# Down projection of fifteen experts by seven block products, in the mixture-of-experts phase of a denoising layer

## The chip, the cores and the metric

The kernel runs on one core of one Trainium2 chip. Its engines work side by side, each through its own list of instructions, and wait for one another by semaphores: TensorE (PE, matmuls into PSUM), ScalarE (ACT), VectorE (DVE), GpSimd (POOL, which also issues the gathers and scatters), and SyncE (SP), which issues most loads. The metric is the device time of one execution of the whole kernel, in microseconds; lower is better.

## The reference, cut to what matters

The layer has a mixer (a long convolution and a retention branch) and then a mixture of experts. Only the experts and the last norm are touched here. `T` is 2048 for the latent tokens and 128 for the context tokens, `D` is 1024, there are 16 experts, and each takes its own best tokens: 256 latent and 16 context ones.

```python
def ec_moe(h, p):
    xt = h.reshape(T, D)
    aff = jax.nn.softmax((xt @ p["w_router"]).astype(F32), axis=-1)
    cap = (EC_CAPACITY_FACTOR * T) // N_EXPERTS
    vals, idx = lax.top_k(aff.T, cap)
    xs = xt[idx]
    hid = jax.nn.silu(einsum("ecd,edf->ecf", xs, w_e_gate)) * einsum("ecd,edf->ecf", xs, w_e_up)
    ye = jnp.einsum("ecf,efd->ecd", hid, p["w_e_down"]) * vals[..., None]
    y = jnp.zeros((T, D)).at[idx.reshape(-1)].add(ye.reshape(-1, D))
# trunk_layer:  x = x + g2 * ec_moe(h, p);   result: rmsnorm(x, norm_f_g)
```

## The kernel before, in words

The kernel has seven phases, one after the other: filters, tokens, hyena input, middle, merge, out, experts. The experts phase (`phase_experts`, L2804) is about the last 1245 us. The merge phase, which the diff leaves alone, has sums of weight and row blocks on GpSimd in its own right (L2401 to L2425) and low parts on VectorE (L2302).

All products with large weights are made from three matmuls of rounded operands (`product`, L71 to L73): each float32 operand is split in a high part, rounded to fp32r, and a low part, the rest. high x high, high x low and low x high are added up in PSUM. ScalarE writes a high part (`split` in the scalar block, L3150), VectorE then the low part (`split` in the vector block, L3374: raw minus high).

An expert has 24 weight rows of 128x1024, streamed in the order of the list `STREAM`: for each f of 8 a gate column g_f, an up column u_f and, one f later, a down row d_f. SP loads them (`loads`). TensorE makes g_f and u_f for 272 slots (`column`, 8 x 3 matmuls of 272 columns each); ScalarE applies silu to g_f (`act_g`, L3197); VectorE multiplies with u_f to the hidden row `full` (L3467, 256 latent slots) and `full_c` (L3468, 16 context slots); ScalarE rounds `full` (L3208) and VectorE takes its low part (L3476), with a split of a weight row between the two. Then `down` (TensorE) adds the row f of the down projection to four PSUM banks: two halves of the slots by two halves of the 1024 output columns, 4 x 3 matmuls of 512 columns for a row, 96 for an expert. The rows 0 to 5 lie between the columns of the same expert; `down_context` (L3093, the 16 context slots straight from the raw rows) follows after u7, and rows 6 and 7 after that. Four gatings on VectorE (L3501: PSUM x routing value x gate) write `ye`, and a context gating (L3489). GpSimd scatters `ye` onto the residual in memory (L3611), waits until it has landed (`carry`, L3535), and then gathers the tokens of the next expert that is due (L3548 to L3557).

Beside this, VectorE counts positions for the expert after the next (`passed`, L3334 and L3337), and it and ScalarE split the transposed tokens of the next expert (`turned`; L3380 and L3383 from PSUM). In the last expert the final norm of all 17 tiles runs between the columns: GpSimd loads tiles of the residual, ScalarE squares them (L3170), VectorE scales them (L3408), GpSimd stores them. This starts when the scatter of expert 14 has landed. The rows which expert 15 itself adds to are gathered, added to and stored at the end (L3414, L3423, L3596).

The order on each engine is written out by hand in its `body`, called 16 times by `experts`. A weight row is split two stream positions ahead of its use (`LEAD`).

## Time and profile before

| | |
|---|---|
| median of three timed runs | 3281.8 us (3281.4 to 3283.2) |
| the profiled execution | 3281.0 us, its span 3279.1 us |
| mean granted TensorE clock | 0.965 of full |
| PE busy | 3086.5 us (94%) |
| DVE busy | 1910.9 us (58%) |
| ACT busy | 1412.6 us (43%) |
| POOL busy | 525.5 us (16%) |
| DMA | 630.7 MB, mean 192 GB/s |

A busy share is the time in which an engine works on an instruction; issuing DMAs and waiting for semaphores is not counted. The span goes from the first to the last instruction. The granted clock is the share of TensorE's full clock that the chip lets it have: 1.00 is 2.4 GHz, 0.50 is 1.2 GHz. The ends of matmuls are modelled, so that the distance between their starts, and not their duration, is the cost of one in a run of them.

### The profile page before, as it was taken

The numbers are of one execution on the slowest core, as the hardware profiler recorded it, in microseconds if no ns is written. First come the engines' busy times: TensorE is split into PE (matmuls) and PEld (weight loads), VectorE is DVE, ScalarE is ACT, GpSimd is POOL, SyncE is SP. The second block draws the span as 40 slices with busy tenths as digits, with TensorE's granted clock in tenths as the row PEclk, the third lists the DMA queues.
The fourth block names the chain that finished last, engine by engine and source line by source line (L and its number), as shares of the span: only waits on it lengthen the run. The fifth ranks groups of instructions, "written<-read, shape, count | busy, mean of one in ns | idle before, by whom it ended". The sixth has DMA issues, their size and how long they took to land. (4 is left out here: it accounts for less than half of the span.)

```text
span 3279.1 us, 52938 instructions
## 1 busy us (share of the span) xinstructions
PE 3086.5 (94%) x20253; PEld 2673.8 (82%) x20253; DVE 1910.9 (58%) x3135; ACT 1412.6 (43%) x2101; POOL 525.5 (16%) x440
## 2 busy tenths in 40 slices
PE   7899999899979879999999994999999999999997
PEld 2478888799945779999997773999999999899996
DVE  5544443433345578776755558666666666666656
ACT  4633333422234145564644541444444444444446
POOL 1011111000023344101000003121111111112212
PEclk9999999999989889999999995999999999999998
DMA  8733332422199976767655443565555555565668
GB/s 332 262 110 119 121 108 88 153 60 63 54 326 357 338 236 219 244 212 236 211 175 196 160 147 120 197 208 201 192 197 195 187 190 182 182 207 194 198 207 310
DMA packets 338341, 630.73 MB, mean 192 GB/s; under 512 B 28408, under 2 KB 209912, under 8 KB 333961
## 3 DMA queue, kind: packets, MB, share of 16 engines
q1 hardware_dynamic: 312159, 568.47, 50.8%
q0 software_dynamic: 16992, 54.88, 5.7%
q10 hardware_dynamic: 8976, 4.46, 0.5%
q8 instruction: 143, 2.34, 0.3%
q14 instruction: 71, 0.58, 0.1%
HBM read 490.16 MB, written 137.56 MB: 191 GB/s over the span
## 5 line engine op out<-in xcount | busy, mean ns | idle before, releaser
L71 PE MATMUL experts_bank<-experts_xT_high,experts_w_high_gu 128*128 128x272 f32 x2048 | 595.4, 291 | 7.5 <-DVE experts_w_low_gu L3374 3.5
L73 PE MATMUL experts_bank<-experts_xT_high,experts_w_low_gu 128*128 128x272 f32 x2048 | 590.7, 288 | 0.0
L72 PE MATMUL experts_bank<-experts_xT_low,experts_w_high_gu 128*128 128x272 f32 x2048 | 588.8, 287 | 0.0
L71 PEld LDWEIGHTS experts_bank<-experts_xT_high,experts_w_high_gu 128*128 128x128 f32 x2048 | 385.5, 188 | 14.0 <-ACT experts_act_g L3197 6.3
L72 PEld LDWEIGHTS experts_bank<-experts_xT_low,experts_w_high_gu 128*128 128x128 f32 x2048 | 386.4, 189 | 4.6
L73 PEld LDWEIGHTS experts_bank<-experts_xT_high,experts_w_low_gu 128*128 128x128 f32 x2048 | 385.3, 188 | 0.0
L3374 DVE TENSOR_TENSOR experts_w_low_gu<-experts_w_raw_gu,experts_w_high_gu 128x1024 fp32r<-128x1024 f32 x256 | 302.3, 1217 | 24.9 <-ACT experts_w_high_gu L3150 20.1
L2145 PE MATMUL merge_bank<-merge_rows_high,merge_w_gates_high 128*128 128x272 f32 x896 | 261.5, 292 | 9.2 <-DVE merge_rows_low L2302 5.9
L3150 ACT ACTIVATE experts_w_high_gu<-experts_w_raw_gu 128x1024 fp32r<-128x1024 f32 x256 | 256.7, 1045 | 13.8 <-DMA experts_w_raw_gu<-in_w_stream 13.8
L2147 PE MATMUL merge_bank<-merge_rows_high,merge_w_gates_low 128*128 128x272 f32 x896 | 260.7, 291 | 0.0
L2146 PE MATMUL merge_bank<-merge_rows_low,merge_w_gates_high 128*128 128x272 f32 x896 | 259.3, 289 | 0.0
L73 PE MATMUL experts_bank<-experts_w_high_d,experts_hid_low 128*128 128x512 f32 x512 | 203.7, 398 | 0.0
L71 PE MATMUL experts_bank<-experts_w_high_d,experts_hid_high 128*128 128x512 f32 x512 | 203.6, 398 | 0.0
L3197 ACT ACTIVATE experts_act_g<-experts_bank 128x272 f32<-128x272 f32 x128 | 50.9, 397 | 352.4 <-PE experts_bank L73 352.4
L72 PE MATMUL experts_bank<-experts_w_low_d,experts_hid_high 128*128 128x512 f32 x512 | 202.3, 395 | 0.0
L3467 DVE TENSOR_TENSOR experts_full<-experts_bank,experts_act_g 128x256 f32<-128x256 f32 x128 | 54.4, 425 | 252.8 <-issue 150.3
L71 PE MATMUL hyin_pz<-hyin_hT_high,hyin_w_high 128*128 128x436 f32 (+1 forms) x480 | 176.3, 367 | 14.0 <-DVE hyin_hT_low L1421 14.0
L2145 PEld LDWEIGHTS merge_bank<-merge_rows_high,merge_w_gates_high 128*128 128x128 f32 x896 | 170.2, 190 | 9.9 <-issue 9.9
L3535 POOL TENSOR_TENSOR experts_spare<-experts_spare 128x1 f32<-128x1 f32 x46 | 29.5, 653 | 920.9 <-DVE experts_ye L3501 772.5
L72 PE MATMUL hyin_pz<-hyin_hT_low,hyin_w_high 128*128 128x436 f32 (+1 forms) x480 | 172.9, 360 | 0.0
L73 PE MATMUL hyin_pz<-hyin_hT_high,hyin_w_low 128*128 128x436 f32 (+1 forms) x480 | 172.9, 360 | 0.0
L2146 PEld LDWEIGHTS merge_bank<-merge_rows_low,merge_w_gates_high 128*128 128x128 f32 x896 | 170.4, 190 | 0.0
(435 smaller groups left out, 7257.9 us busy)
## 6 DMA issues: line engine op xcount, KB each, us to landing
experts_w_raw_gu<-in_w_stream SPq DMA_DIRECT2D x256, 512.0 KB, 4.6
experts_w_raw_d<-in_w_stream SPq DMA_DIRECT2D x128, 512.0 KB, 6.9
merge_rows_b<-scratch_hT SPq DMA_DIRECT2D x52, 544.0 KB, 5.1
filters_wm<-in_w_mod SPq DMA_DIRECT2D x12, 2048.0 KB, 10.8
merge_rows_t<-scratch_row_sums SPq DMA_DIRECT2D x36, 544.0 KB, 6.6
merge_y<-scratch_yhy SPq DMA_DIRECT2D x32, 544.0 KB, 5.1
merge_y<-scratch_yret SPq DMA_DIRECT2D x32, 544.0 KB, 4.6
x_early<-in_xT SPq DMA_DIRECT2D x17, 512.0 KB, 5.1
```

The costliest lines, as they stand in the source:

```text
L71: pe.matmul(out, lhs[0], rhs[0], start=start, stop=False)
L72: pe.matmul(out, lhs[0], rhs[1], start=False, stop=False)
L73: return pe.matmul(out, lhs[1], rhs[0], start=False, stop=stop)
L2145: pe.matmul(out, high, rh[:, w, q, :], start=not onto and q == 0, stop=False, skip_group_check=onto)
L2146: pe.matmul(out, high, rl[:, w, q, :], start=False, stop=False, skip_group_check=onto)
L2147: mm = pe.matmul(out, low, rh[:, w, q, :], start=False, stop=q == HK - 1, skip_group_check=onto)
L3150: act.activation(wh[kind][:, n % RINGS[kind], :], raw[kind][:, r, :], ACT.Copy).then_inc(*AW.inc(name))
L3197: act.activation(act_g[:], pg[:, 0:SLOTS], ACT.Silu).then_inc(*AG.inc(f"g{f}"))
L3374: v.tensor_tensor(wl[kind][:, w, :], raw[kind][:, n % STAGES[kind], :], wh[kind][:, w, :].bitcast(F32), ALU.subtract).then_inc(*VW.inc(name))
L3467: v.tensor_tensor(full[:, f % 2, :], pu[:, 0:CAP], act_g[:, 0:CAP], ALU.mult).then_inc(*VG.inc(f"m{f}"))
L3535: g.tensor_tensor(spare[:, column:column + 1], spare[:, 0:1], spare[:, 0:1], ALU.add)\
```

## The change

For experts 0 to 14 the down projection is made by Strassen's scheme in Winograd's form. The hidden matrix (256 slots by 1024) and the down weight (1024 by 1024) are cut in halves both ways. With A for hidden, B for weight: S1 = A21 + A22, S2 = S1 - A11, S3 = A11 - A21, S4 = A12 - S2; t1 = b12 - b11, t2 = b22 - t1, t3 = b22 - b12, t4 = b21 - t2. The seven products A11 b11, A12 b21, S1 t1, S2 t2, S3 t3, A22 t4, S4 b22 have 4 x 3 matmuls of 512 columns each, 84 for an expert.

- All seven products of expert e are moved behind columns 0, 1, 3, 5, 6, 7 and 8 of expert e+1 (`BEHIND`). Three PSUM banks hold them; four products add onto a bank that is already in use, after ScalarE has copied out its state (`copied`), and VectorE adds and gates the quarters (`evicted`, `summed`, `gated`).
- GpSimd makes t1, t3, t2 and t4 from the raw rows, in place: each is 4 rows of 512 columns, 128x2048 elements (`block_sum`, `quarter`). t1 stands ahead of the gather, the others between the gather and the scatter, which is now that of expert e-1.
- ScalarE and VectorE split 14 operand parts of 2 x 512 (`PARTS`), in the place of 8 rows, in a ring of three (`RING_D`, four before), most of them in expert e+1 (`SPLIT_AT`), three at the end of expert e (`SPLIT_NEXT`).
- VectorE makes S1 to S4 for f of 4 to 7, 16 sums of 128x128, and the low parts of 6 x 128 columns at once; for f of 0 to 3 only A11 (128 columns) is split.
- SP reloads the raw down rows after their last use (`load_row`), at positions 6 to 9 of the next expert.
- Expert 15 keeps the 96 matmuls, with its rows behind columns 11 to 15 and after. The final norm's batches, buffers and positions are changed (`BATCHES`, `SPOT`, `SQUARES`, `SCALED`).
- The context gating takes four pieces straight from PSUM on VectorE and one scaling on ScalarE.

The diff, cut to its core:

```diff
+STREAM = [f"{n}{f}" for f in range(KT) for n in "gu"]
+LEAD, RING, RING_D = 2, 4, 3
+HALF = KT // 2
+OPERANDS = ["b11", "b21", "t1", "t2", "t3", "t4", "b22"]
+PARTS = [f"{name}{i}" for name in OPERANDS for i in range(2)]
+BEHIND = {0: 0, 1: 1, 3: 2, 5: 3, 6: 4, 7: 5, 8: 6}
+SPLIT_AT = {1: [3], 2: [4, 5], 4: [6, 7], 5: [8], 6: [9, 10], 7: [11, 12], 8: [13]}
+SPLIT_NEXT = {13: 0, 14: 1, 15: 2}
+D_FIRST = (1, 6, 7, 8)
...
+        BATCHES = [(0, 4), (4, 8), (8, 12), (12, NT)]
+        SQUARES = {12: (0, 4), 14: (4, 8)}
+        SCALED = {13: (0, 4), 15: (4, 8)}
+        ROWS_AT = {6: (0, 1), 7: (2, 3), 8: (4, 5), 9: (6, 7)}
+        PASSED_AT = {0: (0, 6), 1: (6, 9), 3: (9, 13), 5: (13, NLAT)}
+        DOWN_AT = {11: 0, 12: 1, 13: 2, 14: 3, 15: 4}
...
+                def load_row(e, f):
+                    if e:
+                        sp.wait_ge(VP.sem, VP.at(e - 1, f"{'b22' if f >= HALF else 't3'}{f % HALF // 2}"))
+                        sp.wait_ge(TP.sem, TP.at(e - 1, "t4"))
...
+                def block_product(e, j):
+
+                    to = pd[:, (0, 1, 2, 0, 0, 0, 2)[j], :]
+                    onto = j > 2
...
+                    for i in range(2):
+                        n = 2 * j + i
+                        w = ring_d(e, n)
+                        pe.wait_ge(VP.sem, VP.at(e, PARTS[n]))
+                        for q in (2 * i, 2 * i + 1):
+                            high, low = hh[:, q, j, :], hl[:, q, j, :]
+                            right = slice(512 * (q % 2), 512 * (q % 2) + 512)
+                            pe.matmul(to, high, dh[:, w, right], start=not onto and q == 0, stop=False, skip_group_check=onto)
+                            pe.matmul(to, high, dl[:, w, right], start=False, stop=False, skip_group_check=onto)
+                            mm = pe.matmul(to, low, dh[:, w, right], start=False, stop=q == HALF - 1, skip_group_check=onto)
...
+                        if e and i == 2:
+                            copied(e - 1, 0, "p1")
+                        if e and i == 6:
+                            copied(e - 1, 3, "u2")
+                        if e and i == 7:
+                            copied(e - 1, 4, "u3")
...
+                def summed(e, c, j, name, done):
+
+                    to = {"c11": ye[:, 0, 0:512], "c22": ye[:, 1, 512:DM], "c12": ye[:, 0, 512:DM]}[done]
+                    v.wait_ge(DP.sem, DP.at(e, PARTS[2 * j + 1]))
+                    v.wait_ge(AY.sem, AY.at(e, name))
+                    v.tensor_tensor(to, pd[:, 1 if done == "c11" else 2, :], to, ALU.add).then_inc(*VD.inc(c))
+                    v.wait_ge(VD.sem, VD.at(e, c))
+                    gated(e, to, to, done)
...
+                    v.tensor_tensor(sums[:, 3, :], full[:, q, 0, :], full[:, q, 1, :], ALU.subtract).then_inc(*VG.inc(f"x{f}"))
+                    done("m")
+                    v.tensor_tensor(sums[:, 1, :], full[:, q, 1, :], sums[:, 4, :], ALU.add).then_inc(*VG.inc(f"z{f}"))
+                    done("z")
+                    v.tensor_tensor(sums[:, 2, :], sums[:, 1, :], full[:, q, 0, :], ALU.subtract).then_inc(*VG.inc(f"y{f}"))
+                    done("y")
+                    v.tensor_tensor(sums[:, 5, :], sums[:, 0, :], sums[:, 2, :], ALU.subtract).then_inc(*VG.inc(f"w{f}"))
...
+                def block_sum(e, name):
+
+                    if name == "t1":
+                        for f in range(HALF):
+                            g.wait_ge(dld[f], 16 * (e + 1))
+                        g.wait_ge(PC.sem, PC.at(e, "context"))
+                        g.wait_ge(VP.sem, VP.at(e, "b111"))
+                        to, a, b = quarter("b11"), quarter("t3"), quarter("b11")
...
+                    elif name == "t2":
+                        g.wait_ge(VP.sem, VP.at(e, "t11"))
+                        to, a, b = quarter("t2"), quarter("b22"), quarter("t1")
+                    else:
+                        g.wait_ge(TP.sem, TP.at(e, "t2"))
+                        g.wait_ge(VP.sem, VP.at(e, "b211"))
+                        to, a, b = quarter("t4"), quarter("b21"), quarter("t2")
+                    g.tensor_tensor(to, a, b, ALU.subtract).then_inc(*TP.inc(name))
...
                 def body(e, h, k, one, two):
-                    if final(e):
-                        finish(h)
-                        return
+                    if e:
+                        block_sum(e - 1, "t1")
                     if one:
                         gather(e + 1, 1 - h)
...
+                    if e:
+                        for name in ("t3", "t2", "t4"):
+                            block_sum(e - 1, name)
+                        scatter(e - 1)
+                    if final(e):
+                        finish(e % 3)
```

## Rows read from the trace of the kernel before

**Rows 1.** Windows, one expert each: us, busy of each engine, clock, DMA share, GB/s
```profile
core 0: us, PE busy (x) PEld busy (x) DVE busy (x) ACT busy (x) POOL busy (x), PEclk, DMA share, GB/s
2563.60:2639.90 76.30, 76.30 (x567) 70.01 (x568) 47.91 (x83) 33.48 (x51) 14.87 (x12) 1.00 0.58 196
...
3097.40:3173.50 76.10, 76.10 (x563) 69.82 (x562) 41.63 (x65) 33.32 (x50) 14.00 (x12) 1.00 0.59 196
3173.50:3279.00 105.50, 83.10 (x568) 73.34 (x568) 68.88 (x87) 63.20 (x101) 31.30 (x45) 0.92 0.83 301
```

**Rows 2.** Chain of waits: start us, us, engine, tile, line
```profile
2033.68 0.60 PE experts_bank L71
...
2106.04 0.34 PE experts_bank L71
...
2604.85 0.44 PE experts_bank L3052 x4
2614.09 0.44 PE experts_bank L3052 x4
...
3173.47 0.43 PE experts_bank L71
```

**Rows 3.** Timeline of TensorE in the down rows: start us, us, instruction
```profile
2564.01 0.39 PE L73 MATMUL experts_bank<-experts_w_high_d,experts_hid_low 128*128 128x512 f32 x1
...
2568.91 0.39 PE L73 MATMUL experts_bank<-experts_w_high_d,experts_hid_low 128*128 128x512 f32 x1
```

**Rows 4.** Groups of VectorE, one expert (2563.6 to 2639.9): busy us, mean ns, idle before
```profile
L3374 DVE TENSOR_TENSOR experts_w_low_gu<-experts_w_raw_gu,experts_w_high_gu 128x1024 fp32r<-128x1024 f32 x16 | 18.9, 1218 | 0.0
...
L3476 DVE TENSOR_TENSOR experts_hid_low<-experts_full,experts_hid_high 128x256 fp32r<-128x256 f32 x8 | 3.3, 418 | 0.0
L3501 DVE SCALAR_TENSOR_TENSOR experts_ye<-experts_bank,experts_vals,experts_gate 128x512 f32<-128x512 f32 x4 | 2.8, 749 | 1.0 <-PE experts_bank L73 1.0
L3383 DVE TENSOR_TENSOR experts_xT_low<-experts_bank,experts_xT_high 128x512 fp32r<-128x512 f32 x4 | 2.8, 690 | 7.3 <-ACT experts_xT_high L3162 7.3
...
L3489 DVE SCALAR_TENSOR_TENSOR experts_ye<-experts_ye,experts_vals,experts_gate 16x1024 f32<-16x1024 f32 x1 | 1.3, 1271 | 1.1 <-ACT experts_ye L3217 1.1
...
L3380 DVE TENSOR_TENSOR experts_xT_low<-experts_bank,experts_xT_high 128x128 fp32r<-128x128 f32 x1 | 0.3, 290 | 1.0 <-ACT experts_xT_high L3161 1.0
```

**Rows 5.** Timeline of VectorE in the same expert
```profile
2570.00 2.35 DVE L3374 TENSOR_TENSOR experts_w_low_gu<-experts_w_raw_gu,experts_w_high_gu 128x1024 fp32r<-128x1024 f32 x2
```

**Rows 6.** Groups of ScalarE in the same expert
```profile
L3150 ACT ACTIVATE experts_w_high_gu<-experts_w_raw_gu 128x1024 fp32r<-128x1024 f32 x16 | 16.0, 1044 | 0.0
...
L3208 ACT ACTIVATE experts_hid_high<-experts_full 128x256 fp32r<-128x256 f32 x8 | 3.4, 419 | 16.4 <-DVE experts_full L3467 16.4
```

**Rows 7.** Groups of GpSimd over the span, two sums of the merge phase's first blocks
```profile
L1958 POOL TENSOR_TENSOR merge_rows_b<-merge_rows_b,merge_rows_b 128x1088 f32<-128x1088 f32 x1 | 2.5, 2474 | 0.0
L1948 POOL TENSOR_TENSOR merge_gates_sum<-merge_gates 128x1024 f32<-128x1024 f32 x1 | 2.3, 2342 | 0.0
```

**Rows 8.** Timeline of VectorE in the merge phase, 1362 to 1380
```profile
1365.28 3.11 DVE L2302 TENSOR_TENSOR merge_rows_low<-merge_rows_b,merge_rows_high 128x1088 fp32r<-128x1088 f32 x1 [1.77 <-ACT merge_rows_high L2224]
1368.32 0.77 DVE L2319 TENSOR_TENSOR merge_gate<-merge_bank,merge_sums 128x272 f32<-128x272 f32 x2
...
1378.55 1.28 DVE L2302 TENSOR_TENSOR merge_rows_low<-merge_y,merge_rows_high 128x1088 fp32r<-128x1088 f32 x1
```

**Rows 9.** Timeline of GpSimd over the same stretch
```profile
1364.85 2.39 POOL L2419 TENSOR_TENSOR merge_gates_sum<-merge_gates 128x1024 f32<-128x1024 f32 x1 [74.16 <-DMA merge_gates<-in_w_gates]
1367.32 3.33 POOL L2421 TENSOR_TENSOR merge_gates_sum<-merge_gates_sum,merge_gates 128x1024 f32<-128x1024 f32 x1
```

**Rows 10.** Groups of GpSimd in one expert (2563.6 to 2639.9), the gather's affinity rows
```profile
L3557 POOL DMA_INDIRECT experts_aff_rows<-scratch_aff,experts_ids x3 | 4.0, 1330 | 0.9 <-issue 0.9
```

**Rows 11.** Windows of the merge phase while four sums run on GpSimd (columns as rows 1)
```profile
1205.00:1210.00 5.00, 0.54 (x5) 0.32 (x3) 1.79 (x1) 2.68 (x4) 4.87 (x3) 1.00 0.66 237
1210.00:1215.00 5.00, 3.72 (x16) 3.75 (x17) 5.00 (x6) 2.20 (x3) 5.00 (x2) 0.57 0.64 181
```

**Rows 12.** Timeline of GpSimd in the last expert: the carry behind the scatter
```profile
3195.70 0.19 POOL L3535 TENSOR_TENSOR experts_spare<-experts_spare 128x1 f32<-128x1 f32 x1 [7.50 <-DMA scratch_xacc<-experts_ye,experts_sids]
```

622 lines of the change are left out of this document (378 added, 244 removed).

## The prediction

> **What bounds the kernel now.** I began with the page's busy shares and then left them, since a mean over seven phases says little about one. The first view that counts is the table of windows, one window for each expert [rows 1]. In a middle expert TensorE is busy for all of the 76.3 us at a granted clock of 1.00; VectorE is busy for 47.9 us, ScalarE for 33.5 and GpSimd for 14.9. The chain of waits over the same stretches passes through TensorE alone: the first down product behind the context rows of expert 0 starts at 2106.04 and that of expert 14 at 3173.47, so an expert takes 1067.43 / 14 = 76.25 us [rows 2]. In the timeline the 512-column matmuls of the down projection start 0.233 us apart (21 steps from 2564.01 to 2568.91) [rows 3]. Two transpose groups stand 9.24 us apart in the chain, and between them lie two columns, one down row of 12 matmuls and the transposes [rows 2]: (9.24 - 2.80 - 0.44) / 2 = 3.00 us for one gate or up column. So TensorE is the bound, with no idle time, in experts 1 to 14, and in the last expert it is not: there it is busy for 83.1 of 105.5 us while the final norm runs [rows 1].
>
> **What the change takes from TensorE.** The down projection of an expert has 96 matmuls of 512 columns now (8 rows, 4 outputs, 3 terms). Seven products of 4 rows and 3 terms are 84. 12 x 0.233 = 2.80 us less for each of 15 experts, 42.0 us in all, if TensorE stays the bound: 73.5 us an expert. All else on TensorE (columns, transposes, context, index) is only reordered.
>
> **What it puts on VectorE, for one expert.** The rows are those of one expert's window [rows 4]; an instruction that follows another without a wait costs less than its mean, as two splits take 2.35 us together in the timeline against 1.22 for one [rows 4, 5], so 1.13 each.
> - Weight parts: 14 splits in the place of 8, 6 x 1.13 = +6.8 us.
> - Hidden rows: the low part is 128 wide for four rows and 768 wide for the other four, where it was 256. From 256 to 1024 elements the rows go from 418 to 1218 ns, 1.04 ns an element: 4 x 0.53 - 4 x 0.13 = +1.6 us.
> - Sums of hidden halves: 16 instructions of 128 elements, in a chain of waits on itself. No row has this form with both inputs in SBUF; the nearest is the 128-element subtraction of 290 ns. 16 x 0.29 = +4.6 us (bounds 0.20 and 0.35 each, 3.2 to 5.6).
> - Evictions: 3 additions from PSUM (690 ns by the 512-element subtraction from PSUM) and 4 gatings (749 ns) for 4 gatings now: about +2.3 us with the longer issue of single ones. The context's four pieces of 256 elements (418 ns by the row of that width) replace one of 1271 ns: +0.4.
> Together 47.9 + 15.7 = 63.6 us. To that comes a wait that VectorE has not now: between the product `full` and its low part it ran a weight split while ScalarE rounded, and now the two stand next to each other. ScalarE's 256 elements take 419 ns and 1024 take 1044 [rows 6], so 768 take 0.84 and 128 about 0.3. With 0.1 for the semaphore this is 4 x 0.95 + 4 x 0.3 = 5.0 us. 68.6 us: by itself that would still fit under 73.5.
>
> **The four weight sums on GpSimd decide it.** Each has 128x2048 elements with two inputs in SBUF. The merge phase has such sums: undisturbed, 2342 ns for 1024 and 2474 for 1088 elements [rows 7]. By the slope (2.06 ns an element) 2048 take 4.45 us, by doubling 4.68; I take 4.55, so 18.2 us an expert. What they do to VectorE is seen in two timelines of the merge phase. A VectorE subtraction of 1088 elements takes 1.28 us at 1378.55, when no sum runs. The one that begins at 1365.28, shortly after a GpSimd sum (1364.85 to 1367.24), takes 3.11 us: it ends at 1368.39, 1.15 us after the sum. The next sum starts at 1367.32 and takes 3.33 us instead of 2.34; it ends 2.26 us after that subtraction [rows 8, 9]. So instructions with two SBUF inputs exclude each other on these two engines, each for the whole length of the other. The page "SBUF — State Buffer" of the Trainium skill (Who interferes with whom) adds that a VectorE instruction with one SBUF input is free of this; the trace agrees, since the two of L2319 at 1368.32, which read PSUM, take 0.77 us within the sum [rows 8, 9]. No row has a sum of 2048 elements. The Trainium skill's page "GPSIMD Engine Reference" (Elementwise — side-by-side cycle accounting) gives 4497 ns for one, by which the four would be 18.0 us instead of my 18.2; its section Engine selection says to keep elementwise work off GpSimd, which speaks against this part of the change.
>
> Nearly everything VectorE does here has two SBUF inputs: the 30 splits, the 14 counting steps L3337, the hidden sums, the low parts. Only `full`, the additions from PSUM, the xT parts and the waits for ScalarE can lie beside a sum. All four sums fall in the first half of an expert, by their place: t1 when the context product is over, then the gather of the next expert (three instructions of 1.33 us [rows 10] and three like them, some 8 us with the gaps), then t3, t2, t4 one behind the other. With the durations above, in the order of the code, from TensorE's start of an expert: t1 0.1 to 4.6, VectorE blocked at the last low part of the expert before; then context pieces and numbers to 7.3; split gu2, six counting steps 10.8; splits d3, gu3, three steps 14.3; `full` 0 14.9; t3 14.6 to 19.1, low 0 blocked to 19.4; splits gu4, d4, d5 22.8, gu5 24.0; t2 24.0 to 28.5 (it needs d5), gating c11 blocked to 29.2; t4 29.2 to 33.7, four counting steps blocked to 35.3; `full` 1 35.9. So 15.8 of the 18.2 us are lost and 2.4 lie beside something. u2 needs the PSUM bank that `full` 1 frees: TensorE would take it up at 27.5 and stands for some 8 us. The merge phase has such a place: while its sums run, TensorE is busy 0.54 of 5 us, and the granted clock is 0.57 in the next stretch, most of it at the level of 1.2 GHz [rows 11]. That comes on top and costs a later column up to 3 us. VectorE's own round is then 68.6 + 15.8 = 84.4, and it waits 2 to 3 us for TensorE and ScalarE at the products: **86.5 us an expert** instead of 76.3 (the walk itself, with each row's mean, closes at 88). TensorE's 42 us turn into idle time.
>
> Bounds of this period: 77.5 if the sums lie beside all the waits and all the PSUM reads (8 us beside) and the hidden sums cost 0.2 each; 91 if every stall brings the low clock and TensorE then is late for VectorE in its turn. I take 86.5 by the walk.
>
> **Other edits.** ScalarE gets 6 splits (+6.0), wider rounding (+1.3) and three copies (+1.8) and stays near 43 us; costed at nothing, but its copies p1, u2, u3 stand ahead of its splits, and while one waits for a product the splits behind it wait too; that is in the 2 to 3 us. SP now waits for the last part of b22 and for t4 before it reloads the down rows; behind that wait stand the gate and up loads, which have four columns (12 us) of room: nothing, unless the wait is longer than that; then TensorE waits for a column. The scatter moves from the start of the next expert to about 65 us into it and ends before the next t1: nothing in the middle, but it costs at the end.
>
> **The ends.** Expert 0 does six of its down rows before its context product now (2033.68 to 2106.04, 72.4 us [rows 2]); after the change they go to the next expert: 72.4 - 6 x 2.8 = 55.6. Expert 14 has no counting steps (41.6 against 47.9 us of VectorE [rows 1]): 80.5 us. The last expert takes 105.6 now, from 3173.47. Its final norm starts after the scatter of expert 14, whose carry ends at 3195.9, 22 us in [rows 12]; the two down rows (5.6) and the last gating before it leave some 15 us for the scatter and its landing. After the change it needs the last product of expert 14, at about 59 us, and ends at 74. Then 4 tiles land (5), ScalarE squares them ahead of its next splits (5 to 7), then two columns and rows 4 to 7 of the last down projection follow with stalls (about 25), and after the last product VectorE still has 9 tiles to scale (1.2 each), 3 row groups and 4 gatings (about 27): 74 + 12 + 25 + 27 = 138 us. TensorE's own minimum is 105.6 + 14.0 = 120 (seven products of expert 14 for two rows of it); bounds 122 and 150.
>
> **Sum.** Now the phase takes 72.4 + 1067.4 + 105.6 = 1245.4 us. After: 55.6 + 13 x 86.5 + 80.5 + 138 = 1398.6, +153. On the profiled span 3279.1 that is 3432; the profiled execution lies 1.9 us above its span and 0.8 below the median: 3435 us. With the low bounds (77.5, 73.5, 122) it is 3296, with the high ones (91, 85, 150) 3510.
>
> **Rivals.**
> 1. Faster, with TensorE still the bound. The 4 sums must then cost VectorE less than 73.5 - 68.6 = 4.9 us an expert, and less than 7.7 for any gain in the period at all. For it: VectorE is idle 28 us an expert now, much of it before hidden rows. Against: these gaps are filled by 20 us of new work, and the merge phase shows no sum that costs so little. Its time is 3281.8 - 42 + 18 for the tail = 3258. 12%.
> 2. The exclusion is there, but half of it is hidden, if VectorE runs ahead of TensorE when a sum comes, or if the sums fall on its waits for ScalarE (5 us). For it: t1 comes where VectorE now waits for the last columns. Against: t3, t2 and t4 follow each other, with 11 down splits due in the same 40 us. Period 79: 13 x 79 + 76 + 130 + 56 = 1289, +44: 3326. 15%.
> 3. The gain and the lock cancel: period 75 to 76, within 0.2% of now: 2%.
> 4. The forecast, 83 to 91 an expert, 3385 to 3510 in all: 71%.
> Range: 3315 to 3495 leaves out the faster case (12 to 13%) and the last 7%. About 0.2% (6.6 us) is what a measurement of this kernel tells from no change: faster 0.13, same 0.02, slower 0.85.
>
> **What would show it.** By windows: a middle expert of 86 us, VectorE busy for all but 5 to 8 us of it, TensorE idle 12 or more. By lines: the four sums at 4.5 to 5.8 us each, the 1024-element low splits with a mean well over 1.22 (some at 4 to 5.7). In the waits: TensorE on `full_context` or on the low splits. The granted clock under 1.00 in the first half. Wrong would be: all low splits at 1.22 us while a sum runs, or a period of 73.5 with VectorE under 68 us.

## The result, and the profile after

The changed kernel takes 3534.8 us (median; 3532.1 to 3537.0) against 3281.6 for the kernel before: a ratio of 1.0768, 95% interval 1.0755 to 1.0781. The profiled execution has a span of 3531.7 us and a mean granted clock of 0.941. The forecast was 3435 us with a range of 3315 to 3495: the direction was right, and the size was short by 100 us.

The page of the kernel after: busy time of each engine, then the groups that grew (busy us, mean ns of one | idle before, and what ended it).

```profile
PE 3114.6 (88%) x20073; PEld 2694.8 (76%) x20073; DVE 2381.5 (67%) x3558; ACT 1512.1 (43%) x2184; POOL 805.5 (23%) x500
...
L3493 DVE TENSOR_TENSOR experts_w_low_gu<-experts_w_raw_gu,experts_w_high_gu 128x1024 fp32r<-128x1024 f32 x256 | 312.6, 1221 | 84.6 <-ACT experts_w_high_gu L3241 79.8
L3782 POOL TENSOR_TENSOR experts_w_raw_d<-experts_w_raw_d 128x2048 f32<-128x2048 f32 x60 | 293.7, 4895 | 276.8 <-PE experts_bank L3176 176.0
L3502 DVE TENSOR_TENSOR experts_w_low_d<-experts_w_raw_d,experts_w_high_d 128x1024 fp32r<-128x1024 f32 x210 | 251.2, 1220 | 51.2 <-ACT experts_w_high_d L3256 51.2
```

VectorE now waits 79.8 us for the high parts of the gate and up rows and 51.2 us for those of the down parts. Before, the same splits had an idle time of 0.0 ahead of them [rows 4].

Windows of a middle expert (from one chunk index instruction on VectorE to the next), of expert 14 and of the last expert (these two from the end of one context product on TensorE to the end of the next, the last one to the end of the span): us, busy of PE, PEld, DVE, ACT, POOL, granted clock, DMA share, GB/s.

```profile
2750.53:2843.14 92.61, 78.52 (x555) 71.72 (x554) 79.78 (x112) 40.36 (x56) 33.32 (x16) 0.93 0.50 161
3301.57:3386.60 85.03, 77.48 (x551) 70.15 (x550) 72.21 (x93) 40.44 (x56) 31.61 (x16) 0.96 0.54 173
3386.60:3531.70 145.10, 100.77 (x630) 87.98 (x628) 96.97 (x109) 70.71 (x106) 49.53 (x49) 0.85 0.61 217
```

These answer to [rows 1]. A middle expert took 76.3 us with TensorE busy throughout; now it takes 92.6, TensorE is idle for 14.1 of them, and VectorE has gone from 47.9 to 79.8 us. The same index instruction (the one which, in both kernels, stands at the start of an expert on VectorE) gives a split of the whole difference between the two spans:

| stretch, by that mark | before | after | difference | forecast |
|---|---|---|---|---|
| start to expert 1 | 2106.2 | 2099.3 | -6.9 | -16.8 |
| experts 1 to 13 | 991.4 | 1208.1 | +216.7 (16.7 each) | +133 (10.25 each) |
| experts 14 and 15, to the end | 181.5 | 224.4 | +42.9 | +36.7 |
| span | 3279.1 | 3531.7 | +252.6 | +153 |

So 83 of the missing 100 us lie in the period of the middle experts. How the rest is divided depends on the mark. In the changed kernel VectorE comes to the index instruction of expert 1 5.8 us after TensorE has ended the context product (2093.50 and 2099.28), since the sum t1 holds up the last low part; before, these two were 0.4 us apart (2105.83 and 2106.22). The forecast was made from TensorE's times. By these the start is 12.3 us shorter (forecast 16.8) and the last two experts are 48.2 us longer (forecast 36.7): 4 of the missing us at the start and 12 at the end.

Where VectorE's time goes in the middle expert of 92.6 us, by its groups:

```profile
L3493 DVE TENSOR_TENSOR experts_w_low_gu<-experts_w_raw_gu,experts_w_high_gu 128x1024 fp32r<-128x1024 f32 x16 | 19.5, 1220 | 4.1 <-ACT experts_w_high_gu L3241 4.1
L3502 DVE TENSOR_TENSOR experts_w_low_d<-experts_w_raw_d,experts_w_high_d 128x1024 fp32r<-128x1024 f32 x14 | 16.7, 1220 | 2.9 <-ACT experts_w_high_d L3256 2.9
L3457 DVE SCALAR_TENSOR_TENSOR experts_tally<-experts_pos_slot,experts_tally 128x256 bf16<-128x256 f32 x14 | 15.0, 1127 | 0.0
L3568 DVE TENSOR_TENSOR experts_hid_low<-experts_hid_sums,experts_hid_high 128x768 fp32r<-128x768 f32 x4 | 7.8, 1960 | 3.7 <-ACT experts_hid_high L3329 3.7
L3517 DVE SCALAR_TENSOR_TENSOR experts_ye<-experts_ye,experts_vals,experts_gate 128x512 f32<-128x512 f32 x3 | 5.9, 1957 | 0.1
```

The weight splits (first two rows) are not stretched at all: 1220 ns, as in [rows 4]. What is stretched are the counting steps (1127 ns), the 768-wide low parts (1960) and three gatings (1957). The timeline shows how. First GpSimd, then VectorE, in the first half of the next expert (start us, us, [idle before <- what ended it]):

```profile
2853.65 4.59 POOL L3782 TENSOR_TENSOR experts_w_raw_d<-experts_w_raw_d 128x2048 f32<-128x2048 f32 x1
2864.76 10.41 POOL L3782 TENSOR_TENSOR experts_w_raw_d<-experts_w_raw_d 128x2048 f32<-128x2048 f32 x2 [6.53 <-DVE experts_w_low_d L3502]
```

```profile
2852.81 6.12 DVE L3457 SCALAR_TENSOR_TENSOR experts_tally<-experts_pos_slot,experts_tally 128x256 bf16<-128x256 f32 x3
2858.96 0.42 DVE L3543 TENSOR_TENSOR experts_full<-experts_bank,experts_act_g 128x256 f32<-128x256 f32 x1
...
2861.19 1.23 DVE L3493 TENSOR_TENSOR experts_w_low_gu<-experts_w_raw_gu,experts_w_high_gu 128x1024 fp32r<-128x1024 f32 x1 [1.14 <-ACT experts_w_high_gu L3241]
...
2866.46 4.37 DVE L3517 SCALAR_TENSOR_TENSOR experts_ye<-experts_ye,experts_vals,experts_gate 128x512 f32<-128x512 f32 x1
2870.75 5.90 DVE L3457 SCALAR_TENSOR_TENSOR experts_tally<-experts_pos_slot,experts_tally 128x256 bf16<-128x256 f32 x4
```

The sum from 2853.65 to 2858.24 holds up three counting steps until 2858.93. Of the next pair of sums the first holds up a gating. When, by its length, this sum is through, the gating gets in for its own 0.7 us, and then the four counting steps wait out the second. TensorE, which needs the rows that VectorE makes, stops in its turn. The longest stop ends at 2877.12, and a lower clock follows it, as windows of 5 us show (columns as above):

```profile
2877.12 0.59 PE L71 MATMUL experts_bank<-experts_xT_high,experts_w_high_gu 128*128 128x272 f32 x1 [7.40 <-DVE experts_full_context L3544]
```

```profile
2870.60:2875.60 5.00, 0.00 (x0) 0.00 (x0) 5.00 (x3) 0.00 (x0) 4.58 (x1) 0.80 0.00 0
2875.60:2880.60 5.00, 3.48 (x16) 3.48 (x17) 4.05 (x9) 3.59 (x6) 0.00 (x0) 0.52 0.04 7
```

The wait of 1.14 us at 2861.19 is of the other kind. ScalarE, in the same stretch:

```profile
2848.38 1.04 ACT L3241 ACTIVATE experts_w_high_gu<-experts_w_raw_gu 128x1024 fp32r<-128x1024 f32 x1
2859.41 0.31 ACT L3325 ACTIVATE experts_hid_high<-experts_full 128x128 fp32r<-128x128 f32 x1 [10.00 <-DVE experts_full L3543]
2859.63 0.58 ACT L3263 ACTIVATE experts_ye<-experts_bank 128x512 f32<-128x512 f32 x1
2860.11 1.05 ACT L3241 ACTIVATE experts_w_high_gu<-experts_w_raw_gu 128x1024 fp32r<-128x1024 f32 x1
```

ScalarE stands idle for 10.00 us in front of the rounding of the hidden row, which needs VectorE's product. The high part of the next gate row (2860.11) is behind it in ScalarE's order. If only that order holds it back, it could have been made in those 10 us (a run below tests this). VectorE, the slower of the two, comes to the low part of that row at 2860.05 and waits for it.

The longest wait for a gate row stands at the start of the expert and is of the same kind. Here it is the scaling of the context rows (`ye`, L3337) that needs VectorE's pieces, and the first high gate part is behind it. ScalarE, then VectorE:

```profile
2845.06 1.15 ACT L3337 ACTIVATE experts_ye<-experts_ye,experts_vals 16x1024 f32<-16x1024 f32 x1 [6.97 <-DVE experts_ye L3682]
2846.21 1.04 ACT L3241 ACTIVATE experts_w_high_gu<-experts_w_raw_gu 128x1024 fp32r<-128x1024 f32 x1
```

```profile
2847.28 1.22 DVE L3493 TENSOR_TENSOR experts_w_low_gu<-experts_w_raw_gu,experts_w_high_gu 128x1024 fp32r<-128x1024 f32 x1 [2.26 <-ACT experts_w_high_gu L3241]
```

So of the 4.1 us that VectorE waits for gate rows in an expert, 2.3 stand behind the scaling of the context rows and 1.1 and 0.7 behind the rounding of a hidden row.

### The profile page after: what moved, and what is told of

It is laid out like the page before. It is cut to its first block and busy times, and to the rows that moved or that the text cites. A ratio compares the mean times of both kernels' runs of the same rounds, so it can differ in the third digit from the quotient of the medians.

```text
span 3531.7 us, 53322 instructions
## 1 busy us (share of the span) xinstructions
PE 3114.6 (88%) x20073; PEld 2694.8 (76%) x20073; DVE 2381.5 (67%) x3558; ACT 1512.1 (43%) x2184; POOL 805.5 (23%) x500
## 5 line engine op out<-in xcount | busy, mean ns | idle before, releaser
L71 PE MATMUL experts_bank<-experts_xT_high,experts_w_high_gu 128*128 128x272 f32 x2048 | 619.6, 303 | 116.5 <-DVE experts_full_context L3544 114.1
L72 PE MATMUL experts_bank<-experts_xT_low,experts_w_high_gu 128*128 128x272 f32 x2048 | 607.9, 297 | 0.0
L71 PEld LDWEIGHTS experts_bank<-experts_xT_high,experts_w_high_gu 128*128 128x128 f32 x2048 | 405.5, 198 | 134.9 <-DVE experts_full_context L3544 120.5
L72 PEld LDWEIGHTS experts_bank<-experts_xT_low,experts_w_high_gu 128*128 128x128 f32 x2048 | 405.4, 198 | 5.1
L3493 DVE TENSOR_TENSOR experts_w_low_gu<-experts_w_raw_gu,experts_w_high_gu 128x1024 fp32r<-128x1024 f32 x256 | 312.6, 1221 | 84.6 <-ACT experts_w_high_gu L3241 79.8
L3782 POOL TENSOR_TENSOR experts_w_raw_d<-experts_w_raw_d 128x2048 f32<-128x2048 f32 x60 | 293.7, 4895 | 276.8 <-PE experts_bank L3176 176.0
L3502 DVE TENSOR_TENSOR experts_w_low_d<-experts_w_raw_d,experts_w_high_d 128x1024 fp32r<-128x1024 f32 x210 | 251.2, 1220 | 51.2 <-ACT experts_w_high_d L3256 51.2
L3145 PE MATMUL experts_bank<-experts_w_high_d,experts_hid_high 128*128 128x512 f32 x420 | 176.8, 421 | 76.1 <-DVE experts_w_low_d L3502 76.0
L3256 ACT ACTIVATE experts_w_high_d<-experts_w_raw_d 128x1024 fp32r<-128x1024 f32 x210 | 214.0, 1047 | 0.0
L3457 DVE SCALAR_TENSOR_TENSOR experts_tally<-experts_pos_slot,experts_tally 128x256 bf16<-128x256 f32 x210 | 205.9, 1039 | 0.0
L3147 PE MATMUL experts_bank<-experts_w_high_d,experts_hid_low 128*128 128x512 f32 x420 | 171.9, 409 | 0.0
```

Of the source, the lines that this page charges most:

```text
L71: pe.matmul(out, lhs[0], rhs[0], start=start, stop=False)
L72: pe.matmul(out, lhs[0], rhs[1], start=False, stop=False)
L3145: pe.matmul(to, high, dh[:, w, right], start=not onto and q == 0, stop=False, skip_group_check=onto)
L3457: mm = v.scalar_tensor_tensor(mine, slot[:], at, mine, ALU.is_ge, ALU.add)
L3493: v.tensor_tensor(gl[:, w, :], raw_gu[:, w, :], gh[:, w, :].bitcast(F32), ALU.subtract).then_inc(*VW.inc(STREAM[n]))
L3502: v.tensor_tensor(rows(dl[:, w, :]), part_of(e, n), rows(dh[:, w, :].bitcast(F32)), ALU.subtract)\
```

## The experiments

The theory: VectorE's own round is the period. It is its work, plus the sums that shut it out for their length, plus the waits into which the two hand-written orders of ScalarE and VectorE force it. The rivals: the price of the sums lies in the stalls and low clock of TensorE rather than in VectorE's round; the price depends on where sums stand, not on how long they are; or the products themselves (more splits, sums and waits without any GpSimd) are what costs. All periods below are means over experts 1 to 13 by the mark used above.

**Without the sums.** GpSimd keeps each place, wait and signal, and computes one element a partition; t1 to t4 are then the raw blocks.

```diff
-                    g.tensor_tensor(to, a, b, ALU.subtract).then_inc(*TP.inc(name))
+                    k = 1 + ("t1", "t3", "t2", "t4").index(name)
+                    g.wait_ge(TP.sem, TP.at(e - 1, name))
+                    g.tensor_tensor(token[:, k:k + 1], token[:, 0:1], token[:, 0:1], ALU.subtract).then_inc(*TP.inc(name))
```

> The four sums of 128x2048 on GpSimd are left out (a subtraction of one element a partition stands in their place, with the same waits), so the weight operands t1 to t4 are the raw blocks. Exclusion theory: in the changed kernel VectorE's instructions are stretched by 16.7 us an expert while a sum runs; without them the period falls from 92.9 to 76 to 78 us, the time to about 3315 us (3290 to 3335), and the counting steps, the 768-wide low parts and the gatings are back at 0.48, 0.96 and 0.75 us. Rival, that VectorE's other new work and its waits for ScalarE are the bound and the sums lie in its idle time: period 88 us or more, 3470 us or more.

Measured: 3289.2 us, ratio 1.0021 (1.0011 to 1.0031), 1 us below the range that I had given. The period is 75.9. Window and groups of one expert of it:

```profile
2701.81:2777.66 75.85, 74.23 (x556) 67.97 (x555) 63.06 (x112) 40.37 (x56) 15.91 (x16) 1.00 0.59 197
```

```profile
L3494 DVE TENSOR_TENSOR experts_w_low_gu<-experts_w_raw_gu,experts_w_high_gu 128x1024 fp32r<-128x1024 f32 x16 | 19.5, 1220 | 4.1 <-ACT experts_w_high_gu L3242 4.1
L3503 DVE TENSOR_TENSOR experts_w_low_d<-experts_w_raw_d,experts_w_high_d 128x1024 fp32r<-128x1024 f32 x14 | 16.8, 1220 | 2.9 <-ACT experts_w_high_d L3257 2.9
L3458 DVE SCALAR_TENSOR_TENSOR experts_tally<-experts_pos_slot,experts_tally 128x256 bf16<-128x256 f32 x14 | 5.9, 480 | 0.0
L3569 DVE TENSOR_TENSOR experts_hid_low<-experts_hid_sums,experts_hid_high 128x768 fp32r<-128x768 f32 x4 | 3.8, 958 | 3.7 <-ACT experts_hid_high L3330 3.7
L3518 DVE SCALAR_TENSOR_TENSOR experts_ye<-experts_ye,experts_vals,experts_gate 128x512 f32<-128x512 f32 x3 | 2.3, 752 | 0.1
```

Counting steps are back at 480 ns, 768-wide low parts at 958 and gatings at 752. The sums took 9.1 us from the counting steps, 4.0 from the low parts and 3.6 from the gatings: 16.7 us, VectorE's 79.8 less 63.1. The period fell by 17.0. What the sums held of VectorE appears in full in the period, and only 0.3 us more does, though the clock went from 0.93 to 1.00 and TensorE lost its stops. VectorE's waits for ScalarE (4.1, 2.9, 3.7) are the same with and without sums, so they aren't an effect of them. They also close the account of VectorE: 63.1 of work, 4.1 + 2.9 + 3.7 + 1.2 (before the 128-wide low parts) of waits for ScalarE, 0.4 for TensorE make 75.4 of 75.85 us. TensorE, which has 73.3 us to do, isn't the bound even here.

**Half the sums.** Each of the four over two of its four rows, 128x1024; the other half of t1 to t4 stays raw.

```diff
-                    g.tensor_tensor(to, a, b, ALU.subtract).then_inc(*TP.inc(name))
+                    half = lambda x: x[:, 0:2, :]
+                    g.tensor_tensor(half(to), half(a), half(b), ALU.subtract).then_inc(*TP.inc(name))
```

> The changed kernel, with each of the four GpSimd sums over two of its four rows alone (128x1024 in the place of 128x2048; the other half of t1 to t4 stays raw). Exclusion theory: the cost goes by length. Taking the sums away gave 17.0 us an expert (92.9 to 75.9), so half of their length gives back 7 to 9: period about 85, 3415 us (3395 to 3440). Rival, that each of the four instructions costs by being there (the order of the two engines, the waits between the sums): 92, 3525 us.

Measured: 3400.8 us, 1.0356 (1.0338 to 1.0373), period 84.3. With four sums at the same places, half as long, the cost over the form without them is 8.4 us instead of 17.0. The cost goes by length; a price for each hand-over would have stayed.

**The sums on VectorE.** The four go to VectorE, ahead of the splits at columns 0, 3, 4 and 5.

```diff
+                SUM_AT = {0: "t1", 3: "t2", 4: "t3", 5: "t4"}
...
+                        if e and i in SUM_AT:
+                            block_sum(e - 1, SUM_AT[i])
                         for todo in splits(e, i):
```

> The same four sums, on VectorE in its own order (2.2 to 2.3 us each by 1.04 ns an element) instead of GpSimd. Exclusion theory: 9.1 us of work in the place of 16.7 us of blocked time, 7.6 us less in each of 14 experts: about 3430 us (3400 to 3460), though VectorE has more to do. Rival, that the sums on GpSimd cost VectorE nothing and VectorE is the bound by its own load: 9 us more in each expert, about 3660 us.

Measured: 3374.3 us, 1.028 (1.0263 to 1.0297), period 82.0. I had expected 3430 (3400 to 3460). So this was a miss: the gain is 161 us where I had expected 105.

```profile
L3553 DVE TENSOR_TENSOR experts_w_raw_d<-experts_w_raw_d 128x2048 f32<-128x2048 f32 x4 | 9.2, 2300 | 0.1
```

A sum takes VectorE 2.30 us, where GpSimd takes 4.6 and holds VectorE for nearly all of that. So the work costs less on the engine that is the bound than it does beside it. And of the 9.2 us only 6.1 reach the period: t1 at column 0 fills a wait for ScalarE (the waits of the gate and up splits go from 4.1 to 1.1 us). My forecast had left this wait out, and it makes 3.0 of the 3.3 us an expert by which it was short.

**The same sums beside a VectorE with room.** The kernel before, with eight subtractions of 128x1024 on GpSimd in each of experts 1 to 14, on an idle buffer, at the places of the four sums in GpSimd's order. This adds work and leaves the rest as it was.

```diff
+                    for i in range(2):
...
+                        g.tensor_tensor(spot[:], spot[:], spot[:], ALU.subtract).then_inc(*TP.inc(order[n]))
```

> The kernel before, with eight subtractions of 128x1024 on GpSimd in each of the experts 1 to 14, on a buffer that nothing else uses then, at the places where the changed kernel has its four sums; nothing needs their result. Exclusion theory: some of VectorE's splits take 3 to 3.5 us instead of 1.22, its busy time grows by 12 to 17 us an expert, but it has 28 us of idle time, so TensorE stays the bound: 3282 to 3300 us. Rival, that a sum on GpSimd costs its length wherever it stands: 18 us an expert, 3530 us.

Measured: 3307.1 us, 1.0068 (1.0051 to 1.0085), period 78.2 against 76.3. That is 7 us above the range that I had expected, and far from the rival's 3530. One expert of it, window and GpSimd's group:

```profile
2731.90:2809.87 77.97, 76.48 (x568) 69.97 (x567) 57.48 (x85) 33.25 (x51) 32.57 (x20) 1.00 0.57 191
```

```profile
L3613 POOL TENSOR_TENSOR experts_final_spot<-experts_final_spot 128x1024 f32<-128x1024 f32 x8 | 17.3, 2162 | 0.5
```

17.3 us of sums lengthen VectorE by 9.6 us (57.5 for 47.9) and the expert by 1.9. In the changed kernel 19.5 us of sums lengthen it by 16.7 and the expert by 17.0. Sums hold VectorE in both (two of the splits here take 2.91 us); what differs most is the 28 us of idle time that VectorE had here and doesn't have there. The run doesn't settle whether it matters where the sums fall: they have the same places in GpSimd's list, but not the same times, since these wait for none of VectorE's splits, and t1's place comes 23.1 us behind the mark here and 5.5 us ahead of it there. TensorE waits a little (1.5 us for a low part of the transposed tokens) and makes no stop that brings the clock down (1.00).

**ScalarE's order.** ScalarE makes the high part of the next gate column ahead of the rounding of the hidden row, not behind it. Behind the last hidden row of an expert this puts it ahead of the scaling of the context rows too.

```diff
                         for todo in splits(e, i):
-                            split(*todo)
+                            if i % 2 or todo[0] != "gu" or (e, i) == (0, 0):
+                                split(*todo)
+                        if i % 2 and e * NS + i + 1 < NE * NS:
+                            for todo in splits(*divmod(e * NS + i + 1, NS)):
+                                if todo[0] == "gu":
+                                    split(*todo)
```

> On ScalarE the high part of the next even column is made ahead of the rounding of the hidden row, not behind it. Ordering theory: of the 9.1 us an expert in which VectorE waits for ScalarE's high weight parts some 6 go away, 6 x 14 = 84 us, about 3450 us (3430 to 3475). Rival, that this idle time only covers blocked time and moves elsewhere (the sums alone set the period): 3515 to 3535 us.

Measured: 3471.7 us, 1.0577 (1.056 to 1.0595), period 88.7, 4.2 us less than in the changed kernel. In one expert of 88.7 us (2718.84 to 2807.57) the wait of 4.1 us for the gate and up rows is gone, and the one for the down parts is a little longer:

```profile
DVE experts_w_low_d L3507 <- ACT experts_w_high_d L3256: 3.6, 3, 1.9
```

```profile
L3498 DVE TENSOR_TENSOR experts_w_low_gu<-experts_w_raw_gu,experts_w_high_gu 128x1024 fp32r<-128x1024 f32 x16 | 19.5, 1221 | 0.0
```

No instruction was taken away; the order of ScalarE alone is worth 4.2 us an expert, 63 us in the kernel. I had expected 6 us an expert, and the time lies in the range that I gave (3430 to 3475).

**The wait after the hidden row filled too.** ScalarE's order as in the run before, and VectorE makes the low part of that column between `full` and its low part, as the kernel before did. Once with the sums on GpSimd, once with them on VectorE, once without them.

```diff
+                            if e * NS + i + 1 < NE * NS:
+                                for todo in splits(*divmod(e * NS + i + 1, NS)):
+                                    if todo[0] == "gu":
+                                        split(*todo)
                             low(e, f)
```

> The changed kernel, GpSimd sums kept. ScalarE as in the run with the early high part, and VectorE makes the low part of that column between the hidden row and its low part, where it waited for ScalarE. Ordering theory: beside the 4.2 us that the early high part gave, 3 to 4.5 of the 4.9 us of waits after the hidden rows go away: period 84.5 (83 to 87), 3415 us (3395 to 3450). Rival, that the sums then block more, since VectorE has less idle time for them to fall on: 88, 3460 us.

> Both: the sums on VectorE and the order of the run with the filled waits. VectorE's load is then 63.1 + 9.1 = 72.2 us and TensorE's 73.5, both near the bound: period 74 to 76, 3275 us (3262 to 3300), the tail some 25 us longer than in the kernel before. Rival, that the two loads together with the points where they meet make 78 or more: 3320 us.

> The filled order, and the sums left out as in the run without them (t1 to t4 are raw blocks). VectorE has 63 us, TensorE 73.5 us: if TensorE's own count is right, the period is 73.5 to 74 and the time 3255 to 3262 us: the 2.8 us an expert of the saved matmuls appear in full. Rival, that something else (a wait between products and copies, the clock) holds TensorE above its count: 75.9 as without the fill, 3289 us.

| | us | ratio | period | same sums, order as changed |
|---|---|---|---|---|
| sums on GpSimd | 3453.7 | 1.051 (1.0493 to 1.0528) | 87.4 | 92.9 |
| sums on VectorE | 3323.7 | 1.0124 (1.0107 to 1.0141) | 78.4 | 82.0 |
| no sums | 3253.9 | 0.9904 (0.9888 to 0.9921) | 73.3 | 75.9 |

Windows of one expert of each, in the order of the table:

```profile
2710.21:2796.87 86.66, 75.56 (x557) 69.53 (x556) 79.03 (x112) 41.08 (x56) 32.62 (x16) 0.96 0.52 172
```

```profile
2718.44:2796.63 78.19, 74.17 (x556) 68.08 (x555) 71.32 (x116) 41.18 (x56) 13.79 (x12) 1.00 0.58 191
```

```profile
2756.28:2829.56 73.28, 73.28 (x556) 68.05 (x555) 62.63 (x113) 41.35 (x56) 14.14 (x16) 1.00 0.64 204
```

Without sums TensorE is busy for all of 73.28 us at full clock, and the 13 periods are alike to 0.1 us. That is the 73.5 which the count of matmuls gave: Strassen's saving is real, once VectorE is out of its way. But that kernel leaves the sums out. The two whole forms were both slower than I had expected (3415 and 3275), by 39 and 49 us, and both came out near their rivals (3460 and 3320). With the sums on GpSimd the waits after the hidden rows (4.9 us) are gone, and the period falls by 1.3 us only. The rival's cause, that the sums then hold VectorE for longer, isn't what the trace shows: they hold it for 16.4 us (79.0 of the window less the 62.6 of the run without sums), where it was 16.7. New waits of 1.4, 1.0 and 0.5 us stand in the same window. With the sums on VectorE, its 71.3 us of work and 6.2 us of waits make the period.

The form with the sums on VectorE points further, for its work of 71.3 us would fit under TensorE's 73.3. Its timeline has only 0.4 us of idle time on VectorE in columns 0 to 5, and these waits in an expert, the longest of them (2.2 us) behind column 6:

```profile
DVE experts_w_low_d L3507 <- ACT experts_w_high_d L3256: 3.0, 3, 2.2
DVE experts_hid_sums L3570 <- issue: 1.4, 1, 1.4
DVE experts_xT_low L3603 <- ACT experts_xT_high L3269: 1.0, 2, 0.5
DVE experts_w_low_gu L3498 <- ACT experts_w_high_gu L3241: 0.5, 2, 0.3
```

**Counting steps into the waits.** From there, 7 of the 16 counting steps go from columns 0 to 5 to columns 9 to 12, and with them the one step for the context (`passed_context`). Nothing else is touched.

```diff
-        PASSED_AT = {0: (0, 6), 1: (6, 9), 3: (9, 13), 5: (13, NLAT)}
+        PASSED_AT = {0: (0, 4), 1: (4, 6), 3: (6, 8), 5: (8, 9), 9: (9, 12), 10: (12, 13), 11: (13, 14), 12: (14, NLAT)}
...
-                            if part == 5:
+                            if part == 12:
                                 passed_context(e + 2)
```

> The filled order with the sums on VectorE, and 7 of the 16 counting steps moved from columns 0 to 5, where VectorE has no idle time in the trace of that form, to columns 9 to 12, where it waits 1.40, 0.47, 0.26, 0.27, 0.48 and 0.25 us. Nothing is left out. Theory (VectorE's round, work 71.3 us plus the waits that the order leaves): the 7 steps, 3.1 us, go into those waits, the period falls from 78.3 to 75.5, and the kernel takes 3323.7 - 13 x 2.8 = 3287 us. Rival: the waits of the second half are TensorE's pace and not room, and the period stays at 78 or falls by under 1 us: 3310 to 3324.

Measured: 3282.5 us, 0.9996 (0.9987 to 1.0005), which isn't told from no change, and period 75.3. The steps, 3.1 us by their length, took 3.1 us out of the period, from 78.4.

**The copy first.** In addition ScalarE copies u2 ahead of the rounding of the third hidden row.

```diff
-                        if e and i == 6:
-                            copied(e - 1, 3, "u2")
...
+                            if e and i == 5:
+                                copied(e - 1, 3, "u2")
```

> The same, and ScalarE copies u2 out ahead of the rounding of the third hidden row, not behind it. Nothing is left out. In the form without this TensorE waits 2.0 us an expert for a copy. Theory (in-order hand-overs on ScalarE): 1 to 2 us less an expert than with the counting steps moved alone, 3265 to 3275 us, which would be faster than the kernel before by 0.3 to 0.5%. Rival: the rounding is then late by as much, behind the product, and VectorE waits instead: no change, or up to 1 us an expert more.

Measured: 3273.9 us, 0.9973 (0.9963 to 0.9982), period 74.8. TensorE's wait for the copy (0.9 us) is gone; its wait for a low part goes from 0.5 to 1.2 us, and 0.5 us of period is all that comes of the edit.

**Counting steps ahead of the longest wait.** VectorE still waits 2.19 us for a high down part behind column 6. Five of the steps go there (the line with a minus is that of the run before this one).

```diff
-        PASSED_AT = {0: (0, 4), 1: (4, 6), 3: (6, 8), 5: (8, 9), 9: (9, 12), 10: (12, 13), 11: (13, 14), 12: (14, NLAT)}
+        PASSED_AT = {0: (0, 3), 3: (3, 4), 6: (4, 9), 9: (9, 12), 10: (12, 13), 11: (13, 14), 12: (14, NLAT)}
```

> The form with the copy first, and of the 9 counting steps still in columns 0 to 5 five are moved behind column 6, just ahead of the two down splits of column 7, where VectorE waits 2.19 us for ScalarE. Nothing is left out. Theory (VectorE's round is its work and the waits of the order): 5 steps of 0.42 us fill that wait, and the period falls by 1.2 to 1.5 us from 74.8 and stops at TensorE's own 73.3 to 73.6: 3273.9 - 13 x 1.3 = 3257 us, 3254 to 3260. Rival: the wait of 2.19 us is TensorE's pace (the ring slot of a product comes free late) and passes on to the next split: the period stays at 74.8 and the time at 3270 to 3276.

Measured: 3254.5 us (3253.3 to 3255.7), 0.9914 (0.9901 to 0.9928), period 73.3 in all 13. This form leaves nothing out and is faster than both kernels, than the one before by 0.86%. Window, then VectorE's groups of the down splits and of the sums:

```profile
2753.55:2826.84 73.29, 73.29 (x556) 68.06 (x556) 70.92 (x117) 41.28 (x56) 16.42 (x12) 1.00 0.63 204
```

```profile
L3507 DVE TENSOR_TENSOR experts_w_low_d<-experts_w_raw_d,experts_w_high_d 128x1024 fp32r<-128x1024 f32 x14 | 16.7, 1217 | 1.1 <-ACT experts_w_high_d L3256 1.1
L3558 DVE TENSOR_TENSOR experts_w_raw_d<-experts_w_raw_d 128x2048 f32<-128x2048 f32 x4 | 9.2, 2296 | 0.1
```

TensorE is busy throughout at full clock, and VectorE for 70.9 of 73.3 us. By the mark, the start gives 12.2 us, the 13 periods give 38.8 (991.4 to 952.6), and the last two experts take 23.4 back (204.9 for 181.5): 27.5 us of span. The loss at the end is the part of Strassen's form that no order here mended; a form that keeps the 96 matmuls in expert 14 as well was not tried.

**That form with the sums back on GpSimd.** Same order on every engine, the four sums at the places of the changed kernel.

> The same order of every engine as in the form with five counts at the wait, but the four sums are on GpSimd again, at the places of the changed kernel. Nothing is left out. It asks whether the mended order makes room for the sums beside VectorE, or whether only moving them off GpSimd does. Theory: VectorE's work is 71 - 9.2 = 62 us plus some 17 held by the sums, 79, plus 2 to 3 of waits: a period of 81 to 83, 3350 to 3385 us. Rival: t3, t2 and t4 follow each other on GpSimd and only begin once VectorE has made the splits before them, so that the loss stays a chain in the first half which the order can't fill: 85 to 87 as in the filled form, 3410 to 3450.

Measured: 3427.6 us, 1.0448 (1.043 to 1.0465), period 85.5. I had expected 81 to 83 and 3350 to 3385; these are the rival's numbers. Moving four instructions from VectorE to GpSimd costs 12.2 us an expert and 173 us in all. The window, and a pair of down splits in it that a sum falls on:

```profile
2781.51:2866.86 85.35, 75.84 (x556) 69.79 (x555) 79.17 (x113) 41.16 (x56) 34.51 (x16) 0.96 0.54 175
```

```profile
2790.56 7.02 DVE L3507 TENSOR_TENSOR experts_w_low_d<-experts_w_raw_d,experts_w_high_d 128x1024 fp32r<-128x1024 f32 x2 [0.40 <-ACT experts_w_high_d L3256]
```

VectorE is busy for 79.2 us with 9.2 us less to do: 61.7 of work and 17.5 in which the sums hold it.

## Why the prediction was right or wrong

The bound and where it goes: right. TensorE was the bound and is not any more, and VectorE's round sets the period. The chain of waits has TensorE at 18% and VectorE at 16% of the whole span; before, it had TensorE at 36% and VectorE at 1%.

The steps of the sum for a middle expert:

| step | forecast | measured |
|---|---|---|
| TensorE's own time | 73.5 | 73.3 (run without sums, filled) |
| VectorE's work, undisturbed | 63.6 | 63.1 |
| waits after the hidden rows | 5.0 | 4.9 (3.7 + 1.2) |
| held up by the sums | 15.8 | 16.7 |
| other waits for ScalarE and TensorE | 2 to 3 | 7.9 |
| period | 86.5 | 92.6 |

- **Work.** The additions came out to within 0.5 us: 6 more splits, the hidden sums at 0.282 to 0.293 us against 0.290 forecast, the evictions. The waits after the hidden rows came out in part by a slip: the 0.1 us for the semaphore was left out for the four 128-wide parts, and they measured 0.29 each.
- **The lock.** The exclusion by length, read from two timelines of the merge phase [rows 8, 9], holds: 4 sums of 4.6 us take 16.7 of 18.4 from VectorE. "SBUF — State Buffer" of the Trainium skill (Who interferes with whom) adds that the order of issue decides which side waits, and the trace agrees: the splits, which run ahead of a sum, keep their 1220 ns, and the gatings and counting steps behind its start take the whole length. My sign for the mechanism was wrong in just this point. I looked for stretched 1024-wide low splits, which my own walk through the code had not put behind a sum, and in the middle experts there are none; the stretched ones are those that the order puts behind the start of a sum (in the last run that was a pair of down splits, 7.02 us). Nor did my sign of being wrong, splits of 1.22 us while a sum runs, come about: in a middle expert only t2 meets a split, which began 0.16 us ahead of it and keeps its 1.22, and it is the sum that takes 5.51 us in the place of 4.6.
- **The step that failed** is "it waits 2 to 3 us for TensorE and ScalarE at the products". It was 7.9: 7.0 of them at the high weight parts, 0.4 for TensorE and about 0.5 not attributed. I had named one mechanism, ScalarE's copies standing ahead of its splits, and put it at nothing of its own. The true one is wider. High parts of weight rows stand on ScalarE behind steps that need VectorE. Of the 4.1 us at the gate rows 2.3 stand behind the scaling of the context rows and 1.8 behind the rounding of a hidden row. Of the 2.9 us at the down parts 0.7 stand behind a rounding alone, 1.1 behind a rounding and the copy of u2, and 1.1 behind the copy of u3, the only one that waits for a product. While TensorE was the bound, ScalarE ran ahead of VectorE there, and the splits had 0.0 of idle time [rows 4]. When VectorE is the bound, ScalarE has to wait for VectorE's result, and VectorE, which has no time to spare, then waits for the high part behind it. The run with ScalarE's order changed gives back 4.2 us of it, all of the 4.1 at the gate rows. Costed from the code's order, as I did for `full` and its low part, this step was within reach.
- **The low clock.** I named a cost of up to 3 us for each later column on top. The clock falls as forecast (0.52 after the stop of 7.40 us), but it costs nothing that can be seen: the account of VectorE closes without it, and VectorE waits for TensorE for 0.4 us only. A slower TensorE runs inside VectorE's round.
- **Start.** By TensorE's times 12.3 us shorter instead of 16.8. Of the 4.5 missing, 2.0 lie ahead of the experts: the first index instruction comes at 2023.18, and before it came at 2021.19. For the rest, I had let expert 0 run at TensorE's pace: between 2025 and 2099.3 VectorE waits 5.5 us for high gate and up parts and 3.7 + 0.9 after hidden rows, as in a middle expert.
- **Ends.** Expert 14 took 85.0 us against 80.5, which the same missing waits would explain; the last took 145.1 against 138, and no run took these 7 us apart.
- **The rivals.** The first, that TensorE stays the bound, needed sums that cost less than 4.9 us. They cost 17.0. It would also have failed by the waits: without any sums the period is 75.9. Its 3258 us, from a period of 73.5 and 18 us lost at the end, is 3.5 us from the 3254.5 of the form with the sums on VectorE and the order mended, but that is a kernel other than the one of the diff. The second, half of the lock hidden, fell too: 1.7 of 18.4 us are hidden. It is true of the kernel before, where VectorE has room (9.6 of 17.3 us held, 1.9 paid).
- **What was to be seen.** TensorE idle for 12 or more: 14.1. Sums at 4.5 to 5.8 us: 4.60 to 5.51. TensorE's waits on `full_context` and on low splits: 8.1 and 5.0 us in the expert. VectorE busy all but 5 to 8 us: it was all but 12.8, and this was the sign that told of the missing waits.

## What to carry to other kernels

When a change moves the bound to another engine, cost that engine's round anew from the order of the code: a hand-over with a partner that used to run ahead can become a wait, and here these waits were worth 12 us of a 93 us round, against 17 for the lock that I had looked at so closely. Work with two SBUF inputs put on GpSimd was cheap only where VectorE had idle time to be held in (1.9 us for 17.3 us of sums); where VectorE was the bound, it was better done on VectorE, which took 2.3 us for what GpSimd held it 4.2. Then look for the waits in the bound engine's timeline and put short, free-standing work into them: moving twelve counting steps, one context step and one copy turned a form that was 1.2% slower into one that is 0.9% faster, with not an instruction less.

## What the runs showed of the hardware

- A low clock behind a stall cost nothing in the period while another engine set it: 0.93 in the mean against 1.00 without sums, and the 17.0 us between the two periods are VectorE's 16.7.
- The exclusion is granted at the edge of instructions, and a small one pays the full price: three counting steps of 480 ns took 6.12 us together, and a gating of 0.75 us took 4.37.
- The gather's affinity rows on GpSimd, which read no weights, took longer than before: three of them 5.4 us instead of the 4.0 of [rows 10], one 2.68 us. Neither the sums nor VectorE's busy share accounts for it: over the 13 middle experts the mean of one is 1.80 us in the changed kernel and in the run without sums alike, and 1.37 us in the last run, where VectorE is busy for more of the time. What holds them was not tested.

```profile
2850.95 2.68 POOL L3748 DMA_INDIRECT experts_aff_rows<-scratch_aff,experts_ids  x1 [0.31 <-issue]
```
